# HGRN stage of a hybrid decoder trunk: the block recurrence as four scans, masked values in four buffers, the sample product moved up

## What is computed

```python
def step(S, inp):
    qc, kc, vc, lf = inp
    G = jnp.cumsum(lf, axis=2)
    Gl = G[:, :, -1]
    o_inter = jnp.einsum('bhik,bhkv->bhiv', qc * jnp.exp(G), S)
    ...
    A = jnp.einsum('bhik,bhjk,bhijk->bhij', qc, kc, decay)
    o = o_inter + jnp.einsum('bhij,bhjv->bhiv', A, vc)
    S = S * jnp.exp(Gl)[..., None] + jnp.einsum('bhjk,bhjv->bhkv', kc * jnp.exp(Gl[:, :, None, :] - G), vc)
    return S, o
```

## Time and profile before

| | us |
|---|---|
| median of three runs (2416.15 to 2419.58) | 2416.62 |
| the profiled execution | 2418.88 |
| its span in the trace | 2417.1 |
| HGRN stage of layer 1 (179.9 to 249.3) | 69.4 |
| HGRN stage of layer 2 (1368.1 to 1437.4) | 69.3 |

### The profile page before, as it was taken

The page is one execution under the profiler, slowest core; times in us unless marked ns, Lnnn a source line. Parts: engine busy times, 40 slices in busy tenths (PEclk is TensorE's granted clock), DMA queues, the critical chain, the costliest instruction groups (busy, mean ns, idle before and its releaser), DMA issues. The chain is left out here.

```text
span 2417.1 us, 58486 instructions
## 1 busy us (share of the span) xinstructions
PE 2279.9 (94%) x20484; PEld 2096.0 (87%) x20484; DVE 1522.7 (63%) x3131; ACT 1233.0 (51%) x2351; POOL 1095.9 (45%) x1000
## 2 busy tenths in 40 slices
PE   5987999999999999999979689999999999999998
PEld 4954768999998799999969357799999987999997
DVE  2737634983224968888657466379532268787885
ACT  2540213558556955555536202155675578555554
POOL 0005104984445746566300231078744466565661
PEclk6978899999999999999979789999999999999999
DMA  6566024555553079899544740355565512898993
GB/s 251 167 247 232 3 98 148 183 182 192 191 189 114 0 250 313 286 303 315 176 145 163 270 158 12 132 166 177 187 198 185 190 53 71 284 314 277 306 307 102
DMA packets 123821, 455.53 MB, mean 188 GB/s; under 512 B 13744, under 2 KB 14256, under 8 KB 122544
## 3 DMA queue, kind: packets, MB, share of 16 engines
q1 hardware_dynamic: 105264, 386.80, 45.6%
q0 software_dynamic: 18432, 67.12, 9.9%
HBM read 449.37 MB, written 4.49 MB: 188 GB/s over the span
## 5 line engine op out<-in xcount | busy, mean ns | idle before, releaser
L415 POOL TENSOR_TENSOR parts<-ring,parts 128x512 fp32r<-128x512 f32 x358 | 463.5, 1298 | 472.2 <-ACT parts L408 457.7
L408 ACT ACTIVATE parts<-ring 128x512 fp32r<-128x512 f32 x616 | 386.7, 632 | 363.2 <-PE ps_u L464 280.4
L460 PE MATMUL ps_u<-h_parts,parts 128*128 128x256 f32 x4096 | 563.3, 280 | 1.0 <-ACT parts L408 0.6
L2576 PE MATMUL ps_y<-act_parts,parts 128*128 128x256 f32 x4096 | 562.9, 280 | 0.0
L460 PEld LDWEIGHTS ps_u<-h_parts,parts 128*128 128x128 f32 x4096 | 514.5, 188 | 3.4 <-ACT parts L408 2.0
L2576 PEld LDWEIGHTS ps_y<-act_parts,parts 128*128 128x128 f32 x4096 | 514.4, 188 | 0.9 <-ACT parts L2516 0.7
L415 DVE TENSOR_TENSOR parts<-ring,parts 128x512 fp32r<-128x512 f32 x258 | 177.8, 692 | 385.6 <-ACT parts L408 360.9
L2625 POOL TENSOR_TENSOR act_parts<-big,act_parts 128x256 fp32r<-128x256 f32 x256 | 245.9, 960 | 305.3 <-ACT act_parts L2605 305.3
L464 PE MATMUL ps_u<-h_parts,parts 128*128 128x256 f32 x2048 | 322.4, 280 | 1.4 <-DVE parts L415 1.1
L2580 PE MATMUL ps_y<-act_parts,parts 128*128 128x256 f32 x2048 | 322.5, 279 | 0.0
L464 PEld LDWEIGHTS ps_u<-h_parts,parts 128*128 128x128 f32 x2048 | 275.5, 188 | 2.3 <-DVE parts L415 1.5
(11 more groups left out here) (389 smaller groups left out, 2884.2 us busy)
## 6 DMA issues: line engine op xcount, KB each, us to landing
ring<-in_stream SPq DMA_DIRECT2D x522, 512.0 KB, 4.3
more_ring<-in_stream SPq DMA_DIRECT2D x126, 512.0 KB, 3.7
extra_ring<-in_stream SPq DMA_DIRECT2D x48, 512.0 KB, 5.4
big<-in_stream SPq DMA_DIRECT2D x16, 512.0 KB, 11.7
out_state_out<-big SPq DMA_DIRECT2D x2, 1440.0 KB, 7.1
big<-in_state SPq DMA_DIRECT2D x2, 1280.0 KB, 10.7
big<-in_mixc SPq DMA_DIRECT2D x2, 1024.0 KB, 8.1
big<-in_spots SPq DMA_DIRECT2D x2, 1024.0 KB, 5.4
```

The costliest lines, as they stand in the source:

```text
L408: eng.activation(m.parts[:, q % PARTS, 0, :], half_tile(m, t, half), ACT.Copy).then_inc(s["hi_ready"], 1)
L415: eng.tensor_tensor(m.parts[:, q % PARTS, 1, :], half_tile(m, t, half), m.parts[:, q % PARTS, 0, :].bitcast(F32), ALU.subtract).then_inc(m ...
L460: pe.matmul(out, hi[:, k, :], hr[:, side, kk, 0:tokens], start=(kk + side == 0), stop=False)
L2576: pe.matmul(ps[:, half * KD // 2 + k, :], hi[:, k, :], act_parts[:, j % AHEAD, side, :], start=False, stop=False)
```

## The change

Four things change in `hgrn_block`, all else stays.

1. The states' layout. They were kept block after block, 64 values each; now they are kept with the block as the fast index, 16 blocks for each of the 64 value columns. A half of the prompt (16 blocks) of one pair is 1024 numbers in a row, and one `tensor_tensor_scan` walks it. There are four such scans (2 halves x 2 pairs). The scan's factor is a new array `slow`, the block decays repeated for the 64 columns, made by ACT (`spread_decay`, four 128x1024 copies); its first entry per column is 0, so that the columns don't run into one another. In the second half a 128x64 instruction adds the carried state into PSUM first.
2. The masks. `mask_v` now makes 128x1024 (one head, 16 blocks) eight times instead of 128x512 sixteen times, into four buffers for each half: `vm`, and for the second half memory of gates and start values that are no longer needed, and `sel`. The wait for the products of an earlier turn is gone; a wait for the fifth distance (`products_ready` 5) takes its place.
3. The sample tokens. Their masks are now the first that POOL makes, the product stands on PE between distances 5 and 6, and their four DVE instructions between `values(6)` and `values(7)`.
4. `read_states` now takes weights with a step of 16 numbers (64 bytes) from one column to the next, and there are four of them per pair and half.

The diff, cut to its core:

```diff
+        late = Area(m.big, gates_at).take(2, HD * TB)
+        slow = Area(m.big, gates_at + 4 * A_PAIRS * NT).take(A_PAIRS, HD * TB)
...
+        used = Area(m.big, starts_at).take(HD * TB)
+        spare = m.sel.rearrange("p a b c -> p (a b c)")[:, 0:HD * TB]
...
-        vm = f.take(2, 4, TB // 2, HD)
-        after = f.take(A_PAIRS, BLOCKS, HD)
+        vm = f.take(4, HD * TB)
+        after = f.take(A_PAIRS, 2, HD * TB)
+        decay = f.take(A_PAIRS, BLOCKS)
...
# ACT
+            act.wait_ge(s["decay_ready"], 1)
+            act.wait_ge(s["products_ready"], C)
+            def spread_decay(turn, pair):
+                if turn:
+                    act.wait_ge(s["scan_ready"], pair + 1)
+                act.activation(slow[:, pair, :].rearrange("p (v b) -> p v b", v=HD),
+                               spread(decay[:, pair, turn * TB:(turn + 1) * TB], 1, HD), ACT.Copy).then_inc(s["slow_ready"], 1)
+            spread_decay(0, 0)
+            spread_decay(0, 1)
+            copy_rows(act, m, s, ada_rows, ps_mod, 4)
+            spread_decay(1, 0)
+            copy_columns(act, m, s, ps_mod, 4, 3)
+            spread_decay(1, 1)
...
# POOL
+                for h in (2 * pair, 2 * pair + 1):
+                    i = pool.tensor_tensor(values_of(turn, h).rearrange("p (v b) -> p v b", v=HD),
+                                           spread(vtok[:, turn, h * HD:(h + 1) * HD], 2, TB),
+                                           spread(m.mix("block_rows"), 1, HD), ALU.mult)
...
+            mask_v(0, 0)
+            mask_v(0, 1)
+            pool.wait_ge(s["products_ready"], 5)
+            mask_v(1, 0)
+            mask_v(1, 1)
...
# PE
+            def products(turn, pair):
+                if turn or pair:
+                    pe.wait_ge(s["u_out"], 2 * turn + pair)
+                pe.wait_ge(s["vm_ready"], 2 * turn + pair + 2)
+                for half in range(2):
+                    for r in range(2):
...
+                if d == 5:
+                    sample_products()
+            ada(37, 40)
+            products(0, 0)
+            products(0, 1)
...
+            products(1, 0)
+            turn(3)
+            ada(40, 42)
+            read_states(0, 0)
+            products(1, 1)
+            ada(42, 44)
+            read_states(0, 1)
+            ada(44, 48)
+            read_states(1, 0)
+            mm = read_states(1, 1)
...
# DVE
-                for j in range(TB // 2):
-                    b = turn * TB // 2 + j
-                    for pair in range(A_PAIRS):
-                        new, add = after[:, pair, b, :], ps_outer[:, (2 * turn + pair) % 4, j * HD:(j + 1) * HD]
...
-                            i = ve.scalar_tensor_tensor(new, after[:, pair, b - 1, :],
-                                                        since[:, pair, C * b + C - 1:C * b + C], add, ALU.mult, ALU.add)
+            for turn in range(2):
+                for pair in range(A_PAIRS):
+                    ve.wait_ge(s["u_ready"], 2 * turn + pair + 2)
...
+                    if turn:
...
+                        link(ve.scalar_tensor_tensor(first, last, since[:, pair, C * b + C - 1:C * b + C], first,
+                                                     ALU.mult, ALU.add))
+                    ve.wait_ge(s["slow_ready"], 2 * turn + pair + 1)
+                    link(ve.tensor_tensor_scan(after[:, pair, turn, :], slow[:, pair, :], add, 0.0, ALU.mult, ALU.add))
```

More of the change, by code:

```diff
@@ L996, in hgrn_block, with values_of, sample_values @@
         o = m.mixed[:, 0:2, :]
+        def values_of(turn, h):
+            if turn == 0:
+                return vm[:, h, :]
+            return late[:, h, :] if h < 2 else used if h == 2 else spare
+        def sample_values(h):
+            return flat(after[0:NB * NS, 1, :, :])[:, h * NB * HD:(h + 1) * NB * HD]
         def blocks(x, sample, lo, hi):
@@ L1128, in _ @@
                 ada(*((26, 28), (28, 30), (30, 32), (32, 33), (33, 35), (35, 37))[d - 2])
-            def inter(pair, r, t, n, state):
-                rows = slice(r * HD, (r + 1) * HD)
-                return pe.matmul(ps_sums[rows, pair, t:t + n], state[rows], qt[rows, pair, t:t + n], start=True, stop=True)
-            def read_states(turn):
-                pe.wait_ge(s["scan_ready"], turn + 1)
-                for b in range(turn * TB // 2 + 1, min((turn + 1) * TB // 2 + 1, BLOCKS)):
-                    for pair in range(A_PAIRS):
-                        for r in range(2):
-                            mm = inter(pair, r, C * b, C, after[:, pair, b - 1, :])
-                return mm
@@ L1144, in _ @@
-            for step in range(4):
-                tt = step // 2
-                pe.wait_ge(s["vm_ready"], step + 1)
+                if d == 5:
[3 more added lines that the diff above has]
+            products(0, 1)
+            pe.wait_ge(s["qt_ready"], 1)
+            pe.wait_ge(s["values_done"], 1)
+            for b in range(NB):
                 for pair in range(A_PAIRS):
-                    n = 2 * step + pair
-                    if n >= 4:
-                        pe.wait_ge(s["u_out"], n - 3)
@@ L1167, in _ @@
-                if step >= 2:
-                    read_states(step - 2)
-                    ada(38 + 2 * step, 40 + 2 * step)
-            ada(46, 48)
-            read_states(2)
-            pe.wait_ge(s["vm_ready"], 5)
-            pe.wait_ge(s["u_out"], 8)
-            for pair in range(A_PAIRS):
-                for r in range(2):
-                    rows = slice(r * HD, (r + 1) * HD)
-                    mm = pe.matmul(ps_outer[rows, pair, :], ktt[0:NB * NS, 2, pair, rows], vm[0:NB * NS, 0, 2 * pair + r, :, :],
-                                   start=True, stop=True)
@@ L1237, in _ @@
                 s["gates_ready"], 1)
+            ve.wait_ge(s["gates_ready"], 1)
+            link(ve.tensor_copy(decay[:, :, :], blocks(since, False, C - 1, C).squeeze(3)))
+            for turn in range(2):
+                link(ve.memset(decay[:, :, turn * TB:turn * TB + 1], 0.0))
+            ve.sem_inc(s["decay_ready"], 1)
             for d in range(2, C):
@@ L1240, in _ @@
                 values(d - 1)
[L1241 to L1257 removed]
+            ve.wait_ge(s["u_ready"], 1)
             for pair in range(A_PAIRS):
```

97 lines of the change are left out of this document (48 added, 49 removed).

## The result

The changed kernel ran in 2454.4 us (median of 4 runs, 2449.93 to 2462.46), the kernel before beside it in 2416.68 (2416.15 to 2419.58). The ratio is 1.0151, with a 95% interval of 1.0133 to 1.0169. The forecast was 2414.5, with a range up to 2426.5: the time lies far outside it, on the slow side.

What follows compares the result with a forecast made beforehand. PE's chain, nearly as long as DVE's, was taken to set the stage's end. 0.6 + 0.4, say 1.1 us less a layer, 2.2 in both, gave 2416.7 profiled and 2414.5 us median; range 2405.5 to 2426.5.

Steps and rivals of the forecast that it cites:

- What bounds the stage: HGRN stage: DVE and PE chains almost equally long; shortening DVE's alone uncovers PE's after about 1.5 us.
- The scans: DVE's block walk: four scans at 2.33 us each; DVE's part falls from 20.8 to some 10 us, covered by PE.
- The readings: PE's readings of states near the stage's end: 64 records in 1.97 us each, at 2.4 GHz.
- a rival, at 0.27: PE's stepped weight loads: 1.75 times as long, 1.45 us more a reading, 5.7 us a layer, 2426 us; chance 0.27.
- the forecast's chain: PE from first products to stage end: products, readings, ada tiles and turn, all at 2.4 GHz, ending at 247.3.
- The masks: POOL's 128x1024 masks each hold DVE's SBUF instructions off for 1.65 us; `pairs(7)` done at 222.6, 8.8 us later.
- one is let in behind each mask: DVE up to the end of `pairs(6)`: eight SBUF-only instructions, one entering after each POOL mask, done at 219.8.
- "no hold" rival: DVE beside POOL's masks: held no longer than before, or masks much quicker; 6 us less a layer, 2404.5 us; chance 0.16.
- Behind `pairs(7)`: PE after `pairs(7)` at 222.6: distance 7 until 223.1, five ada tiles 2.3 us, then first products.
- last turn: PE at the stage's end: 0.64 instead of 1.07 us, since the clock need not have fallen.
- low end: Stage end at 246.0 with 1.5 us a mask and the clock back early; 2412 us.
- The clock stays up: PE keeps 2.4 GHz through the barrier into the next stage, some 2 us less a layer, 2410.5 us; chance 0.08.

Runs made afterwards that it cites:

- combined versions: Changed kernel with ACT-turned states, sample work at the end, second-half masks after the last distance: 2415.78 and 2414.4 us; two other ada-tile orders: 2423.31 and 2421.44 us.

## Why the prediction was wrong, point by point

**What bounds the stage: right.** With the walk gone the end is PE's chain; DVE waits 12.27 us for it at the end, and with contiguous weights that chain took 21.7 us against the 21.9 that the forecast's terms make (225.4 to 247.3). The chain's terms at 2.4 GHz were right.

**The scans: right.** The slope of two scans in the earlier trace rows gave 2.29 us, the forecast took 2.33, and 2.29 were measured; the operand in PSUM adds nothing. Carries 0.33 (0.35), ACT's copies 1.05 to 1.10 (1.06).

**The readings: the step that failed.** The sum took 1.97 us for each, and the price with a step stood only in a rival, at 0.27. The rival's mechanism came true, and its size was too small: 1.65 us more a reading instead of 1.45 (a factor 1.84, where it took 1.75), which is 6.4 us for the four of a layer with 5.7 forecast. And it left out what follows: with the slow readings PE's clock falls, and the work between them (products, ada tiles) takes another 3.3 us. Together that is 9.7 us in layer 1 against the run with contiguous weights, and 9.5 against the forecast's chain (31.4 against 21.9). No row of before had a stepped weight load, and I let the missing row speak for the contiguous one. The Trainium skill (SBUF — State Buffer, the note on cachelines) had the direction: each new line of 16 bytes costs. The runs agree at 2.4 GHz, with 3.60 / 1.94 = 1.86 for the weight loads, and with 1.94 / 1.10 = 1.8 for ACT's copy. At 1.2 GHz they show no cost of the step (56 ns a load against 55).

**The masks: mechanism right, size too small.** The 192-element instructions took 2.02 and 1.99 us (forecast 2.0), a mask 1.94 (1.7 to 2.05), the hold is 1.66 for each (1.65). But `pairs(7)` came 10.8 us later instead of 8.8. The step that failed is "one is let in behind each mask": with the masks' starts and lengths shown for POOL, the one of 5.47 us was passed over at the ends of three masks and let in at the fourth, 207.2. The "no hold" rival (0.16) fell.

**Behind `pairs(7)`: the second step that failed.** The forecast put 2.8 us between the end of `pairs(7)` and the first products: distance 7 at once, and five ada tiles at 2.4 GHz. It took 10.7 (222.99 to 233.69). The forecast took PE to be free when `pairs(7)` is done. It is free in neither kernel. In the kernel before, `pairs(7)` was done at 213.81, and PE started distance 7 only 2.5 us later:

```profile
213.68 0.80 PE L1098 MATMUL ps_sums<-big 128*128 128x128 f32 x2
...
216.27 0.69 PE L1098 MATMUL ps_sums<-big 128*128 128x64 f32 x2
...
218.37 1.94 PE L1153 MATMUL ps_outer<-big 128*64 128x512 f32 x8
```

`pairs(5)` to `pairs(7)` follow one another within 3.3 us in both kernels, faster than PE makes the distances and the ada tiles between them. Now the sample product stands in that queue too. When `pairs(7)` is done PE is just starting it: 3.6 us for the product, 2.6 for distance 6 with its two tiles, and 4.6 instead of 2.8 for distance 7 and the five tiles, since most of them run at 1.2 GHz. The forecast had counted the sample product as hidden and PE's clock as back. The earlier trace rows showed 1.2 GHz after a thin stretch, and that entered only the range's end.

These three and the last turn make the sum: forecast -1.1; masks +2.0, behind `pairs(7)` +7.9, readings with the clock +9.5, last turn at 1.2 GHz +0.4, together 18.7, as measured in layer 1. The forecast's low end has a slip that decides nothing: an end at 246.0 instead of 247.3 is 2.6 us in both layers, not 4.

**The clock stays up (0.08): fell,** as the end ran at 1.2 GHz (0.59 from 247 on). It doesn't hold with contiguous weights either: PE kept 2.4 GHz to the end of the stage there, and the first matmuls of the next stage took 0.99 and 1.55 us all the same, as before (0.99 and 1.54). The 0.4 us that the forecast gave the last turn were there in the four stages of the two runs with contiguous weights (0.64 us), but of the eight stages of the combined versions only one has them (0.64; the others 0.96 to 1.07).

What stays open: why POOL lets DVE in behind one mask and not behind another; when exactly the clock falls in such a chain, since it did in some executions with contiguous weights too; and whether the combined version is faster, since its stages are 5.2 and 8.8 us shorter in two profiles and its medians 1.2 and 3.2 us, within what can be told.

## What to carry to other kernels

When a new layout makes one engine's long chain a single instruction, look at who reads the result and with what step: here the scan saved DVE 10 us of which PE had waited for 1.5, and its layout cost PE, which sets the stage's end, 9.7. A price for which no row exists is a price to measure or to avoid (four copies on an idle ACT avoided it). Masks or other long POOL work should be laid where DVE reads PSUM, not moved together ahead of a chain of SBUF instructions that PE waits for. And before a stage's order is changed, see on the trace whether the engine that is to take the work is free at that moment: PE was 2.5 us behind `pairs(7)` even before the sample product came on top.

## What the runs showed of the hardware that I had not expected

- A weight load with 64 bytes from one number to the next takes 56 ns at 2.4 GHz (64 of them 3.60 us) and at 1.2 GHz (120 of them in 6.71 us). Contiguous ones take 30 and 55 ns. So the step costs what a fall of the clock costs, and not both.
- ACT reading 1024 numbers with that step: 1.94 us against 1.10.
- POOL can hold a DVE instruction over several of its own: 5.47 us for one of 32 elements, 8.70 for one of 384.
- PE's clock can fall while PE is busy without a gap: 0.59 on average from 247 to 266, behind a reading with stepped loads, where the same chain with contiguous loads kept 2.4 GHz in four stages of four. In the combined versions, which load contiguously too, it fell at the fourth products in five stages of eight.
